# First modulation worked in two halves, with four weight slabs between them

## The reference

```python
shift_c, scale_c, gate_c = jnp.split(silu_cc @ w_mod[l] + b_mod[l], 3, axis=-1)
hc = modulate(ctx, g_pre[l], shift_c, scale_c)   # rms_norm(ctx, g) * (1 + scale) + shift
zc = split_cols(hc @ w_in[l], IN_SIZES)
```

## Time and profile before

| | us |
|---|---|
| median of 3 runs | 2080.15 |
| lowest, highest run | 2077.9, 2083.12 |
| span of the profiled execution | 2081.5 |
| TensorE busy in the span | 1949.3 (94%) |
| GpSimd busy | 1368.9 (66%) |
| ScalarE busy | 1095.3 (53%) |

### The profile page before, as it was taken

How to read it: one execution, slowest core, us unless ns; L and a number is a source line. 1 busy time by engine, 2 the same in 40 slices (tenths; PEclk the granted TensorE clock), 3 DMA queues, 4 the chain that set the end, 5 groups by cost and what they waited for, 6 DMA issues and landing times.

```text
span 2081.5 us, 26149 instructions
## 1 busy us (share of the span) xinstructions
PE 1949.3 (94%) x9524; PEld 1569.8 (75%) x9524; DVE 595.7 (29%) x1123; ACT 1095.3 (53%) x1571; POOL 1368.9 (66%) x573
## 2 busy tenths in 40 slices
PE   6998999998899979989989999999999989999997
PEld 3776887776668768767878777788888867788886
DVE  3214303424303262351226121331112532132111
ACT  3545644445534654465455685554445586555443
POOL 2755687854558668447869644488887844468884
PEclk8999999999999999999999999999999999999999
DMA  9643465543576536335646433256554633345653
GB/s 343 204 136 121 134 191 171 172 121 112 184 263 209 178 112 192 102 90 172 189 129 184 143 92 101 98 178 192 181 190 138 200 94 96 106 142 174 189 181 112
DMA packets 170816, 328.66 MB, mean 158 GB/s; under 512 B 12384, under 2 KB 13536, under 8 KB 170464
## 3 DMA queue, kind: packets, MB, share of 16 engines
q1 hardware_dynamic: 167968, 320.49, 50.0%
q10 hardware_dynamic: 2752, 6.84, 0.9%
HBM read 326.24 MB, written 1.05 MB: 157 GB/s over the span
## 4 chain that ended last, share of the span: by engine, by line
PE 42%; issue 29%; POOL 25%; ACT 3%; POOLq 1%; DVE 1%; DMA 0%; DVEq 0%; ACTq 0%
POOL wlo L467 25%; PE G L1435 9%; PE G L1437 9%; PE G L1436 9%; PE A L1435 3%; PE A L1437 3%; PE A L1436 3%; ACT whi L481 1%; PE A L1489 1%; ACT t L547 1%; PE A L1817 0%; PE A L1816 0%; PE A L1815 0%; ACT L843 0%; PE G L1877 0%
## 5 line engine op out<-in xcount | busy, mean ns | idle before, releaser
L467 POOL TENSOR_TENSOR wlo<-raw,whi 128x1024 fp32r<-128x1024 f32 x568 | 1365.2, 2411 | 690.0 <-ACT whi L481 686.0
L481 ACT ACTIVATE whi<-raw 128x1024 fp32r<-128x1024 f32 x568 | 599.5, 1058 | 677.5 <-PE G L1437 554.5
L1435 PE MATMUL G<-whi,hhi 128*128 128x512 f32 (+1 forms) x1648 | 662.5, 402 | 21.5 <-DVE hlo L949 9.3
L1437 PE MATMUL G<-whi,hlo 128*128 128x512 f32 (+1 forms) x1648 | 645.2, 392 | 0.0
L1436 PE MATMUL G<-wlo,hhi 128*128 128x512 f32 (+1 forms) x1648 | 644.7, 391 | 0.0
L1435 PEld LDWEIGHTS G<-whi,hhi 128*128 128x128 f32 x1648 | 313.8, 190 | 103.1 <-issue 28.8
L1437 PEld LDWEIGHTS G<-whi,hlo 128*128 128x128 f32 x1648 | 313.4, 190 | 66.5
L1436 PEld LDWEIGHTS G<-wlo,hhi 128*128 128x128 f32 x1648 | 314.3, 191 | 60.1
L1435 PE MATMUL G<-whi,ohi 128*128 128x512 f32 x240 | 94.9, 396 | 1.9 <-ACT gates L494 1.4
L1436 PE MATMUL G<-wlo,ohi 128*128 128x512 f32 x240 | 93.7, 390 | 0.0
L1437 PE MATMUL G<-whi,olo 128*128 128x512 f32 x240 | 93.5, 390 | 0.0
(11 more groups left out here) (360 smaller groups left out, 2262.7 us busy)
## 6 DMA issues: line engine op xcount, KB each, us to landing
raw<-in_w_in SPq DMA_DIRECT2D x332, 512.0 KB, 3.7
raw<-in_w_up SPq DMA_DIRECT2D x64, 512.0 KB, 3.7
raw<-in_w_down SPq DMA_DIRECT2D x64, 512.0 KB, 3.5
raw<-in_w_out SPq DMA_DIRECT2D x40, 512.0 KB, 4.0
raw<-in_w_branch_out SPq DMA_DIRECT2D x36, 512.0 KB, 4.3
modw<-in_w_mod SPq DMA_DIRECT2D x32, 512.0 KB, 3.9
raw<-in_w_branch SPq DMA_DIRECT2D x24, 512.0 KB, 3.5
modz<-in_w_mod SPq DMA_DIRECT2D x16, 512.0 KB, 11.2
```

The lines of the kernel that those rows point to most:

```text
L467: pool.tensor_tensor(wlo[:, s], raw[:, s], whi[:, s].bitcast(F32), ALU.subtract).then_inc(lo_ready, 1)
L481: act.activation(whi[:, slot], raw[:, slot], ACT.Copy).then_inc(hi_ready, 1)
L1435: pe.matmul(bank, hi, whi[:, slot, kk, 0:n], start=first, stop=False)
L1437: return pe.matmul(bank, lo, whi[:, slot, kk, 0:n], start=False, stop=last)
```

## The change

The order of the first layer's w_mod blocks becomes 0, 2, 1, 3, 4, 5, so that the first two hold shift and scale of k-tiles 0 to 3. After these two, TensorE transposes k-tiles 0 to 3 and turns both blocks, VectorE makes the first half of modT (`shift_scale_half`) and both token engines work the first half. The slabs of the first two chunks are put in another order (`FIRST_SLABS`): the upper 512 rows of both chunks, then the lower 512 rows. TensorE works slabs 0 to 2, the eight pieces of blocks 1 and 3, slab 3, then the second half of transposes and turning, and slabs 4 to 15. Gate pieces stand behind slabs 5 to 12, and the two gate blocks are turned after slab 15. ScalarE has copies of blocks 1 and 3 after the split of slab 2, then the split of slab 3, then the loads of the tables; the load of x comes after the third chunk is evacuated. The wait of `mod_turn` for the copy is written out where it is called. The second chunk pair is in the list and only slabs 16 to 23 are left of the former loop, written out.

```diff
+        HB_START = [A[2], A[3], A[1], A[2]]
+        MOD_BLOCKS = [0, 2, 1, 3, 4, 5]
+        FIRST_SLABS = [(0, 0), (0, 1), (1, 0), (1, 1), (0, 2), (0, 3), (1, 2), (1, 3)]
+        FIRST_SLABS += [(c, q) for c in (2, 3) for q in range(SLOTS)]
...
@@ SyncE
-            for _ in range(4 * SLOTS):
+            for _ in range(2 * SLOTS):
                 mod_slab()
...
+                    for i, (c, q) in enumerate(order):
+                        slab(flat["w_in"], l * D + q * SLAB_K * P, first[c], i % SLOTS)
+                        if n == 0 and i == 2:
+                            for _ in range(2 * SLOTS):
                                 mod_slab()
+                        if n == 0 and 6 <= i < 6 + 2 * SLOTS:
+                            mod_slab()
...
@@ ScalarE
-                    for c in range(4):
-                        mod_copy((A[0], A[1], G[0], G[1])[c], modrow[:, c])
-                        if c == 2:
-                            tables(l)
-                            act.dma_start(x[:], g["x"][0].rearrange("(t p) d -> p t d", p=P)).then_inc(x_in, 16)
+                    for c in range(2):
+                        mod_copy(A[c], modrow[:, c])
                     split(0)
                     split(1)
                     act.wait_ge(modT_ready, w(modT_ready))
...
                 if n == 0:
+                    turned_high(scaled, shifted, (0, 1), HB_START)
                     split(2)
+                    for c in range(2, 4):
+                        mod_copy(A[c], modrow[:, c])
                     split(3)
+                    tables(l)
+                    act.wait_ge(modT_ready, w(modT_ready))
+                    turned_high(scaled, shifted, (2, 3), HB_START)
...
+                def evacuate_first(p, dst, slots):
+
+                    for slot in slots[:-1]:
+                        act.wait_ge(weights_used, w(weights_used))
+                        split(slot)
+                    for t in range(TT):
+                        act.wait_ge(projected, w(projected))
+                        act.activation(dst[t], G[2 * p + t][:], ACT.Copy).then_inc(evacuated, 1)
+                    split(slots[-1])
...
+                elif n == 0:
+                    evacuate_first(0, columns(z, RK), (0, 1, 2, 3, 0, 1))
...
+                elif n == 0:
+                    evacuate_first(1, columns(z, RQ), (2, 3))
...
@@ VectorE
+            def shift_scale_half(bank, l, half):
+
+                for c in range(2):
+                    ks = slice(4 * half, 4 * half + 4)
+                    bias = bmodT[:, l, c * KT + 4 * half:c * KT + 4 * half + 4].unsqueeze(2).to_broadcast([P, 4, 2])
+                    ins = dve.tensor_tensor(modT[:, c, ks], mod_ps(bank, 4, c * KT + 4 * half), bias, ALU.add)
+                link(ins)
+                return dve.scalar_tensor_tensor(modT[:, 1, ks], modT[:, 1, ks], 1.0,
+                                                gpreT[:, l, ks].unsqueeze(2).to_broadcast([P, 4, 2]), ALU.add, ALU.mult)
...
@@ TensorE
+                    for c in range(2):
+                        for _ in range(SLOTS):
+                            mod_slab(A[c])
+                    pe.wait_ge(consts_in, w(consts_in, 16 * N_CONST))
+                    pe.wait_ge(norm_ready, w(norm_ready, TT))
+                    turn_tokens(normed, None, (0, 1), HB_START)
+                    for c in range(2):
+                        pe.wait_ge(mod_copied, w(mod_copied))
+                        mod_turn(A[0], 8 * MOD_BLOCKS[c], modrow[:, c], c == 1)
+                    pe.sem_inc(evacuated, 2 * TT)
+                    pe.wait_ge(evacuated, w(evacuated, 2 * TT))
+                    for i, (c, q) in enumerate(FIRST_SLABS):
+                        if i == 4:
+                            pe.wait_ge(mod_copied, w(mod_copied))
+                            turn_tokens(normed, None, (2, 3), HB_START)
+                            mod_turn(A[0], 8 * MOD_BLOCKS[2], modrow[:, 2], False)
+                            pe.wait_ge(mod_copied, w(mod_copied))
+                            mod_turn(A[0], 8 * MOD_BLOCKS[3], modrow[:, 3])
+                        if c >= 2 and q == 0:
+                            pe.wait_ge(evacuated, w(evacuated, TT))
+                        slab(G[2 * (c % 2):2 * (c % 2) + 2], hhi, hlo, q, fresh=c == 0, slot=i % SLOTS)
+                        if i == 2:
+                            for b in range(2, 4):
+                                for _ in range(SLOTS):
+                                    mod_slab(A[b])
+                        if 5 <= i < 5 + 2 * SLOTS:
+                            mod_slab(A[2 + (i - 5) // SLOTS])
+                        if i == 7:
+                            turn_ws()
...
```

More of the change, by code:

```diff
@@ L383, in mod_slab @@
                 c, q = divmod(r, SLOTS)
+                if l == 0:
+                    c = MOD_BLOCKS[c]
                 src = flat["w_mod"][l * D + q * SLAB_K * P:l * D + (q + 1) * SLAB_K * P, c * CH:(c + 1) * CH]
@@ L412, in _ @@
                 if full:
[L413 to L416, removed]
+                    first = [RK, RQ, DKc, DQ]
+                    order = FIRST_SLABS if n == 0 else [(c, q) for c in range(4) for q in range(SLOTS)]
+                    for i, (c, q) in enumerate(order):
+                        slab(flat["w_in"], l * D + q * SLAB_K * P, first[c], i % SLOTS)
+                        if n == 0 and i == 2:
+                            for _ in range(2 * SLOTS):
                                 mod_slab()
+                        if n == 0 and 6 <= i < 6 + 2 * SLOTS:
+                            mod_slab()
                     for c in [RV, DV] + LATE:
@@ L529, in norm, with turned_high @@
                 act.activation(rms[:, 0:TT], ss[:, 0:TT], ACT.Sqrt, bias=eps[:], scale=1.0 / D).then_inc(rms_ready, 1)
-            def turned_high(scale, shift):
-                for q in range(4):
+            def turned_high(scale, shift, qs=range(4), banks=HB):
+                for q in qs:
                     act.wait_ge(h_turned, w(h_turned))
                     for k in range(2 * q, 2 * q + 2):
-                        part = HB[q][:, (k % 2) * S:(k % 2 + 1) * S]
+                        part = banks[q][:, (k % 2) * S:(k % 2 + 1) * S]
                         if shift is None:
@@ L643, in _ @@
                 a = 0 if is_x else 1
-                turned_high(lambda k: modT[:, 1, k, a:a + 1], lambda k: modT[:, 0, k, a:a + 1])
+                scaled, shifted = (lambda k: modT[:, 1, k, a:a + 1]), (lambda k: modT[:, 0, k, a:a + 1])
                 if n == 0:
+                    turned_high(scaled, shifted, (0, 1), HB_START)
                     split(2)
+                    for c in range(2, 4):
+                        mod_copy(A[c], modrow[:, c])
                     split(3)
+                    tables(l)
+                    act.wait_ge(modT_ready, w(modT_ready))
+                    turned_high(scaled, shifted, (2, 3), HB_START)
+                else:
+                    turned_high(scaled, shifted)
                 def decays(heads):
@@ L685, in _ @@
                     pass_by(1)
+                elif n == 0:
+                    evacuate_first(1, columns(z, RQ), (2, 3))
                 else:
-                    evacuate(1, columns(z, RQ if full else RV), ACT.Copy)
+                    evacuate(1, columns(z, RV), ACT.Copy)
                 if n == 0:
-                    mod_copy(A[3], moddrop[:, 1])
                     decays((2, 3))
@@ L714, in _ @@
                     evacuate(0, columns(z, DKc), ACT.Copy)
+                if n == 0:
+                    act.dma_start(x[:], g["x"][0].rearrange("(t p) d -> p t d", p=P)).then_inc(x_in, 16)
+                    mod_copy(A[2], moddrop[:, 0])
                 if n == 2:
@@ L723, in _ @@
                     evacuate(1, columns(z, DQ if full else DV), ACT.Copy)
+                if n == 0:
+                    mod_copy(A[3], moddrop[:, 1])
                 if full:
@@ L937, in norm, with turned_low @@
                     dve.tensor_scalar(normed[:, t], src[:, t], rstd[:, t:t + 1], None, ALU.mult).then_inc(norm_ready, 1)
-            def turned_low(scale, shift):
-                for q in range(4):
+            def turned_low(scale, shift, qs=range(4), banks=HB):
+                for q in qs:
                     dve.wait_ge(h_high, w(h_high))
-                    parts = [(k, HB[q][:, (k % 2) * S:(k % 2 + 1) * S]) for k in range(2 * q, 2 * q + 2)]
+                    parts = [(k, banks[q][:, (k % 2) * S:(k % 2 + 1) * S]) for k in range(2 * q, 2 * q + 2)]
                     if shift is not None:
@@ L1116, in _ @@
             for n, (is_x, l, full) in enumerate(PASSES):
+                a = 0 if is_x else 1
+                scaled, shifted = (lambda k: modT[:, 1, k, a:a + 1]), (lambda k: modT[:, 0, k, a:a + 1])
                 if n == 0:
[L1118 to L1122, removed]
+                    for part in range(2):
+                        dve.wait_ge(mod_turned, w(mod_turned))
```

(27 more changed lines are left out.)

8 lines of the change are left out of this document (3 added, 5 removed).

## The result

The changed kernel takes 2088.57 us in the median of 12 runs (2083.6 to 2094.59), the kernel before 2080.2 (12 runs, 2073.46 to 2085.57). The ratio is 1.0046, 95% interval 1.0035 to 1.0058: 9.6 us slower (7.3 to 12.1); the medians themselves lie 8.4 us apart. Of the two profiled executions the one before took 2083.12 us and the one after 2094.59, the longest of its twelve, so the traces differ by more than the medians do. The forecast was 2085.1 in a range of 2077.5 to 2090.5. The sign of its sum was right, its size about half; and the class that I held likeliest, a difference under 0.3%, is not what came: the interval lies above 1.003.

A forecast was written before the change was run, and what follows sets the result against it. TensorE, busy 94%, was taken as the bound, the opening alone leaving idle time. Slab 4 +0.4, low clock +1.65, pieces +3.1, gate rows +0.9, slab 12 stall -1.1: +5.0 us, 2085.1, range 2077.5 to 2090.5.

The forecast's parts named there:

- Steps 1 to 9: Opening up to slab 4: slab 0 starts 16.5 us earlier, at 29.0; slab 4 at 61.4 against 61.03.
- step 3: Before slab 0: three small VectorE operations take 0.65 us for the old 0.47; slab 0 starts at 29.0.
- steps 6 and 9: ScalarE splits slabs 3 and 4 only behind a copy and the tokens; TensorE idles 4 us, then 6 us.
- three times 1.65 in the sum: Slabs 0, 3 and 4 each begin at the low clock after TensorE idled, 1.65 us more per slab.
- Step 11: Slabs 8 to 11 carry a piece each, 14.1 us, to 91.0; the pieces hide ScalarE's decays block before slab 12.
- Steps 12 and 13: Slabs 12 to 15 end at 102.8, gate rows take 2.9 us, slab 16 starts at 105.7, slab 23 ends at 127.7.
- (a): Rival: the clock stays high through the new idle stretches of TensorE; 0.0 us, 2080; chance 0.12.
- (b): Rival: ScalarE's order does not bind, slab 3 starts at 43.6, slab 4 with its tokens; -3 us, 2077; chance 0.08.
- (c): Rival: the eight pieces before slab 3 let the clock fall; up to +6.5, in all +11.5 us, 2091.5; chance 0.2.
- (d): Rival: halves do not help the start, slab 0 waits for raw data until about 36; 2092; chance 0.04.

The follow-up runs named there:

- e2: The changed kernel with slab 3 split on ScalarE ahead of the copies of row blocks 1 and 3: 2084.79 us, ratio 1.0025 to the kernel before.
- e3: e2 with slabs 4 and 5 also split before ScalarE waits for the second half of modT: 2081.54 us, ratio 1.0014 to the kernel before.
- e4: The changed kernel with unread identity transposes added, 24 before slab 3 and 36 before slab 4: 2084.64 us, ratio 1.0033 to the kernel before.
- e5: The changed kernel with SyncE's gate pieces issued two slabs later, behind raw slabs 8 to 15: 2087.29 us, ratio 1.0037 to the kernel before.
- e9: e8 with slabs 12 and 13 split before ScalarE waits for the decays, 14 and 15 at the third chunk's evacuation: 2074.48 us, ratio 0.9979.
- e1: The kernel before with only the tables loaded after the split of slab 3 and x after the third chunk's evacuation: 2077.22 us, ratio 0.9992.
- e7: The changed kernel with the sum of scale and bias left in PSUM: 2089.08 us, ratio 1.004 to the kernel before.
- e6: The changed kernel with the two gate blocks turned after slab 19 instead of after slab 15: 2085.89 us, ratio 1.0029 to the kernel before.
- e8: e3, e6 and e7 together, with three gate pieces worked in the wait before slab 4, the others behind slabs 5 to 9: 2079.43 us, ratio 0.9993.

## Why the prediction was right, and where it was short

- **Steps 1 to 9**, the head start and its loss, came out within 1.1 us at each landmark from slab 3 to slab 8, in part by luck, since errors inside them cancelled. Turning took 1.84 instead of 2.5. VectorE's 0.65 in step 3 was 2.7, as its last operation stood behind GpSimd; I had weighed that lock for the tokens ("VectorE's second half of the tokens may wait"), not for the small operation in front of them. Slab 0 ran wholly at the low clock and cost 5.3, not 4.4; the eight pieces took 3.66, not 4.7; slab 4 took 5.1, not 4.4, which is most of the 0.8 at slab 8. e2 and e3 take the waits of steps 6 and 9 away and the time follows.
- **The low clock** after the new waits, three times 1.65 in the sum, is shown by e4 for slabs 3 and 4; for slab 0 the rows show it (0.50), and no run took it away by itself. The three cost 2.5, 1.7 and 2.4 us over the 2.75 of a fast slab. The Trainium skill's rule weighed there, "TensorE: Matmul & The Clock Gate", HAM oscillation, that each burst begins at half clock, fits slabs 0 and 4. Slab 3 differs: its first three products ran at granted clock 1.00 (48.60 to 49.40), and the clock fell behind them (0.51 from 49.50 to 53.00).
- **Step 11 failed.** It said that the decays block "moves with the end of slab 7 (by 1 us at most) and its splits end by 90.7". The block's first exponential behind slab 7 moved by 3.6 us, from 76.35 to 79.92, and the split of slab 12 from 86.12 to 89.97, so slab 12 started at 93.60 instead of 91.0 (0.8 of that was there at slab 8). 2.2 us of the shift are the end of slab 7 itself, which came that much later and not 1 us at most (the piece behind it starts at 76.70 against 74.54); 1.4 are the wait for raw slab 11. I had cleared SyncE's order by the distance to the slab's use on TensorE; but ScalarE works its list in order, and the late split of slab 11 held the decays behind it. e5 shows that even without this wait the block ends only 0.2 us earlier, since VectorE's decays then collide with GpSimd. e9 shows what takes it off the path: splitting ahead of it.
- **Steps 12 and 13 were short by 3.3 us**, all of it clock. The wait before slab 12 was not in the sum at all, and the one in the gate turning only with its length. Behind each of them TensorE ran a slab at 0.50 to 0.55: 16.37 us instead of 14.7 from slab 12 to slab 16, and 23.66 instead of 22.0 for slabs 16 to 23.
- In sum, forecast 5.0 against 11.0 in the traces: 0.8 up to slab 8, 1.8 before slab 12, 1.7 and 1.7 for the clock.
- **Rivals.** (a) fell: the clock did fall. (b) was about right on the price (8 us between its sum and mine, 7 in e3), and the code doesn't allow it, as said. (c) put the slow clock in the wrong place: the pieces ran fast (3.66 us for eight); the slow slabs were 0, 3, 4, 12 and 16. Its weight was the right warning for the upper side. (d) fell at 29.89.

## What to carry to other kernels

A head start in front of in-order engines is worth nothing until each engine's list is read for what now stands behind the new waits; here two splits in the wrong place, with the slow slabs behind them, gave back 8.5 of the 15.6 us by slab 4, and the work that had moved between slab 0 and slab 4, with the wait for the second half of the tokens, gave back the rest. Price a wait on TensorE as its length and, with a good chance, another 1.6 to 2.5 us of low clock. When a transfer or a split is brought forward, look at which VectorE operation with two inputs in SBUF it will now meet.

## What the runs showed of the hardware that I had not expected

The granted clock after a wait of 1 to 3.5 us does not follow from the wait's length. Before slab 12 (behind slabs 8 to 11) TensorE waited 1.06 us in e1, 1.10 in the kernel before, 1.65 in e5, 1.88 in e7, 2.42 in e2 and 3.47 in e4, and ran on at 1.00. It waited 1.76 in e3, 1.81 in the changed kernel, 1.93 in e6 and 3.00 in e8, and the slab took 4.5 us (5.25 in e8) at about half clock. Slab 14 in e9 waited 1.78 and ran at 1.00. The wait of 1.12 in the gate turning was followed by the low clock in five of six traces and not in e7. What decides between the two is open; I made no run for it. Only one trace stands behind each figure.

The profile's clock figure is no guide at the very start. From 10 to 22 us it reads 1.00 in the traces before and after, while a piece that takes 0.64 us alone later took 1.08. In e7 it reads 1.00 on through slab 0, which took 5.05 us. Durations beside it tell more there.

VectorE's operations with two SBUF inputs take 0.17 or 0.69 us alone and up to 2.4 or 2.9 beside GpSimd's subtraction, for one full subtraction each. In a chain of such operations each can lose once.
